# Weighted inputs of a bidirectional state-space scan: backward direction on ScalarE, forward on GpSimd

## The reference

```python
w_end = jnp.exp(cum[:, :, -1:] - cum) * dtc
states = jnp.einsum("bcjgn,bcjge,bcjgep->bcgepn", bc, w_end, xc)
chunk_decay = jnp.exp(cum[:, :, -1])
...
return h * dec[..., None, None] + st, h        # the scan over the chunks
```

## Time and profile before

| | |
|---|---|
| median of 3 runs | 1362.33 us (1358.07 to 1363.33) |
| profiled execution, device time | 1359.37 us |
| its span (first to last instruction) | 1357.5 us |
| mean granted clock of TensorE | 0.982 of full |
| busy: TensorE, VectorE, ScalarE, GpSimd | 1298.8, 545.5, 596.5, 603.1 us |
| the stage of the ten products | from 298.0 to 311.1 us of the span |

### The profile page before, as it was taken

The page is one execution under the profiler, slowest core; times in us unless marked ns, Lnnn a source line. Parts: engine busy times, 40 slices in busy tenths (PEclk is TensorE's granted clock), DMA queues, the critical chain, the costliest instruction groups (busy, mean ns, idle before and its releaser), DMA issues.

```text
span 1357.5 us, 17575 instructions
## 1 busy us (share of the span) xinstructions
PE 1298.8 (96%) x6464; PEld 1046.4 (77%) x6464; DVE 545.5 (40%) x1069; ACT 596.5 (44%) x961; POOL 603.1 (44%) x502
## 2 busy tenths in 40 slices
PE   8999999898989999999999899999899999999998
PEld 1688888666777888888888788767678888888886
DVE  2577652668445444443542362783520000001113
ACT  3712555767335344433323464785452222223231
POOL 0335232367143444444665732455424444445562
PEclk9999999999989999999999899999989999999999
DMA  9427457050233445454423312111202222222221
GB/s 393 172 88 285 169 164 133 1 187 1 77 141 124 185 185 193 185 216 179 155 93 98 135 64 92 56 30 57 93 32 93 93 96 106 107 93 93 93 93 62
DMA packets 27401, 166.76 MB, mean 123 GB/s; under 512 B 2976, under 2 KB 5280, under 8 KB 8656
## 3 DMA queue, kind: packets, MB, share of 16 engines
q1 hardware_dynamic: 25328, 151.31, 31.2%
q10 hardware_dynamic: 2016, 14.68, 2.9%
HBM read 163.85 MB, written 6.32 MB: 125 GB/s over the span
## 4 chain that ended last, share of the span: by engine, by line
PE 82%; DVE 7%; ACT 4%; DMA 3%; POOL 2%; issue 1%; SPq 0%; ACTq 0%; DVEq 0%; POOLq 0%
PE bank L274 53%; PE bank L333 12%; PE bank L310 6%; DMA ada_ring<-ada_dram 2%; PE bank L712 1%; PE bank L1349 1%; DVE ada_ring L1987 1%; PE bank L1321 1%; DMA w_raw<-w_dram 1%; PE bank L522 1%; DVE arena L2052 1%; PE bank L536 1%; POOL arena L940 1%; ACT arena L760 1%; PE bank L688 1%
## 5 line engine op out<-in xcount | busy, mean ns | idle before, releaser
L267 POOL TENSOR_TENSOR w_lo<-w_raw,w_hi 128x512 fp32r<-128x512 f32 x336 | 457.3, 1392 | 604.2 <-ACT w_hi L258 604.2
L274 PE MATMUL bank<-h_hi,w_hi 128*128 128x512 f32 x1120 | 442.3, 395 | 12.5 <-DVE h_lo L449 6.9
L274 PE MATMUL bank<-h_lo,w_hi 128*128 128x512 f32 x1120 | 439.2, 392 | 0.0
L274 PE MATMUL bank<-h_hi,w_lo 128*128 128x512 f32 x1120 | 439.0, 392 | 0.0
L258 ACT ACTIVATE w_hi<-w_raw 128x2048 fp32r<-128x2048 f32 x88 | 168.6, 1916 | 299.9 <-PE bank L274 177.1
L274 PEld LDWEIGHTS bank<-h_hi,w_hi 128*128 128x128 f32 x1120 | 212.3, 190 | 57.8 <-issue 8.1
L274 PEld LDWEIGHTS bank<-h_hi,w_lo 128*128 128x128 f32 x1120 | 212.3, 190 | 44.8
L274 PEld LDWEIGHTS bank<-h_lo,w_hi 128*128 128x128 f32 x1120 | 212.4, 190 | 43.0
L2316 DVE TENSOR_TENSOR arena<-arena,bank 128x512 f32 (+1 forms) x22 | 15.1, 687 | 210.2 <-PE bank L274 210.2
L2178 DVE TENSOR_TENSOR h_lo<-arena,h_hi 128x1024 fp32r<-128x1024 f32 x22 | 32.4, 1486 | 135.1 <-ACT h_hi L1813 123.6
L2006 DVE SCALAR_TENSOR_TENSOR arena<-bank,params,arena 128x511 f32<-128x511 f32 (+1 forms) x36 | 25.4, 704 | 136.0 <-ACT arena L1793 114.3
(11 more groups left out here) (276 smaller groups left out, 1756.4 us busy)
## 6 DMA issues: line engine op xcount, KB each, us to landing
w_raw<-w_dram SPq DMA_DIRECT2D x92, 1024.0 KB, 4.8
ada_ring<-ada_dram SPq DMA_DIRECT2D x30, 1024.0 KB, 4.8
ada_ring<-ada_dram ACTq DMA_DIRECT2D x14, 1024.0 KB, 4.9
arena<-ada_dram SPq DMA_DIRECT2D x4, 1024.0 KB, 10.1
arena<-x_dram SPq DMA_DIRECT2D x2, 2048.0 KB, 11.6
bias_copies<-bias_rows SPq DMA_DIRECT2D x1, 4096.0 KB, 17.4
arena<-bias_copies SPq DMA_DIRECT2D x4, 768.0 KB, 5.7
ada_ring<-rpb_dram SPq DMA_DIRECT2D x16, 128.0 KB, 9.5
```

Of the source, the lines that this page charges most:

```text
L267: last = nc.gpsimd.tensor_tensor(w_lo[b % 2][:, part], w_raw[b % 2][:, part], w_hi[b % 2][:, part], ALU.subtract)
L274: last = nc.tensor.matmul(bank[:, :], w[:, ft, k, :], x[:, k, :], start=k == first and m == 0, stop=k == final and m == 2)
```

## The change

GpSimd makes the forward products alone (five instead of ten). The backward ones are made by ScalarE at the head of `ssd_act`, one ACTIVATE for each head (128x64, Copy, with the head's weight column as scale), eight per chunk, 40 in all. A new semaphore `xw_back` counts them. TensorE's order of the ten groups is the same; it waits for `xw` or `xw_back` by the direction. ScalarE waits for `st` at 2k before it writes `xw[1]` again, and L1058 and all behind it follow the 40 instructions.

```diff
@@ ssd_pool
-            for n in range(10):
-                d, c = n % 2, ORDER[n % 2][n // 2]
-                if n >= 2:
-                    pool.wait_ge(sd["st"], n - 1)
-                w = wend[:, d, c * 8:(c + 1) * 8].unsqueeze(2).to_broadcast([P, 8, 64])
-                nc.gpsimd.tensor_tensor(heads(xw[d]), heads(xtok[:, c, :]), w, ALU.mult).then_inc(sd["xw"], 1)
+            for k in range(5):
+                c = ORDER[0][k]
+                if k:
+                    pool.wait_ge(sd["st"], 2 * k - 1)
+                w = wend[:, 0, c * 8:(c + 1) * 8].unsqueeze(2).to_broadcast([P, 8, 64])
+                nc.gpsimd.tensor_tensor(heads(xw[0]), heads(xtok[:, c, :]), w, ALU.mult).then_inc(sd["xw"], 1)
@@ ssd_pe
-                pe.wait_ge(sd["xw"], n + 1)
+                pe.wait_ge(sd["xw_back" if d else "xw"], k + 1)
@@ ssd_act
+            act.wait_ge(sd["wend"], 3)
+            for k in range(5):
+                c = ORDER[1][k]
+                if k:
+                    act.wait_ge(sd["st"], 2 * k)
+                for h in range(HEADS):
+                    part = slice(64 * h, 64 * h + 64)
+                    last = nc.scalar.activation(xw[1][:, part], xtok[:, c, part], ACT.Copy, scale=wend[:, 1, c * 8 + h:c * 8 + h + 1])
+                last.then_inc(sd["xw_back"], 1)
```

More of the change, by code:

```diff
@@ L202, in build @@
                                               "ptr", "pt_act", "pt_dve", "pv", "ohi", "olo")}
-        sd = {n: sem(f"ssd_{n}") for n in ("tr", "tok", "cs", "col", "wend", "xw", "st", "stf", "cb", "cbf", "bc",
+        sd = {n: sem(f"ssd_{n}") for n in ("tr", "tok", "cs", "col", "wend", "xw", "xw_back", "st", "stf", "cb", "cbf", "bc",
                                            "rows", "dmin", "dexp", "z", "t", "both", "m", "y", "yf", "yz", "sq", "mean", "root", "yn", "hi", "lo")}
```

## The result

The changed kernel takes 1364.68 us (median of 20 runs, 1360.97 to 1368.84), the kernel before 1360.80 us in 20 runs beside them. The ratio is 1.0025, with a 95% interval of 1.0015 to 1.0035: slower by 2.0 to 4.8 us, less than 0.5%. The profiled execution has a span of 1364.1 us, 6.6 us over that of the earlier trace rows, which is more than the medians say; the trace tells how much of it is the change's.

A forecast was written before the change was run, and what follows sets the result against it. GpSimd's products and TensorE's groups in turn were taken as the bound; a late start plus four turns of 3.19 us gave +3.1 us, so 1362.5 on the profiled time, 1365.4 on the median, forecast 1364.5 us, range 1360 to 1369.5.

The forecast's parts named there:

- the stage: From the start of the last L578 to the first decay instruction; the fifth backward group in it was forecast 3.1 us later.
- The product's price: Eight ScalarE ACTIVATEs of 128x64 for one backward product: 2.0 us, range 1.76 to 2.1.
- The turn: Backward cycle over the single buffer xw[1]: product 2.0, to TensorE 0.04, group 1.13, back 0.02, 3.19 us in all.
- The late start: ScalarE is free only at 298.29 us, so the first backward group starts at 300.33 instead of about 299.
- The forward turn: GpSimd's forward product, TensorE's group and the waits: 2.3 to 2.7 us, fitting inside 3.19 at no cost.
- The covers: L1058, moved behind the 40 ACTIVATEs, ends at 313.7 us, before the last group (314.2); no cost, cover 0.5 us.
- Rival A: ScalarE's product takes under 1.38 us, so VectorE limits these products: -1.0 us, 1358.4 to about 1361; chance 0.08.
- Rival B: Neighbouring ACTIVATEs on ScalarE do not overlap: product 2.73 us, +6.75 us, 1366 to 1369; chance 0.06.
- Rival C: TensorE's clock falls during these groups: +5.9 to +10.9 us, 1365 to 1370, up to 1373 on the median; chance 0.07.
- Rival D: The shift is swallowed in the chain behind these products: 1359.4 to 1362 us; chance 0.06.

The follow-up runs named there:

- e4: The changed kernel, but GpSimd makes the first backward product too and ScalarE the other four; stage 15.60 us, ratio 0.9983 to the kernel before.
- e3: The changed kernel with two buffers in turn for the backward products; stage 14.36 us, ratio 0.9995 to the kernel before.
- e11: The changed kernel with GpSimd making both first products and two backward buffers (e3 and e4 together); stage 13.22 us, ratio 1.0005 to the kernel before.
- e2: The changed kernel with one ACTIVATE of 128x512 per backward product instead of eight; stage 13.22 us, ratio 1.0000 to the kernel before.
- e8: The changed kernel with four more ACTIVATEs ahead of each backward product, 12 in all; stage 23.02 us, ratio 1.0047 to the kernel before.
- e1: The changed kernel with eight more ACTIVATEs ahead of each backward product, 16 in all; stage 30.34 us, ratio 1.0100 to the kernel before.
- e6: The kernel of e4 run once more; stage 15.60 us, ratio 0.9997 to the kernel before.
- e7: The changed kernel with GpSimd making both first products and two buffers for both directions; stage 14.16 us, ratio 0.9987 to the kernel before.
- e9: The kernel before with two ScalarE copies into dead buffers ahead of the first decay instruction; stage 15.21 us, ratio 1.0022 to the kernel before.

## Why the prediction was right, point by point

- *The forecast.* 1364.5 us, +3.1 us for the stage; measured 1364.68 us, +3.9 us between medians and +3.3 in the stage. The sign and the size hold, and that it stays under 0.5%. The agreement of the time to 0.2 us is luck: the forecast stood on some 1361.4 us for the kernel before, which is 0.6 over the 1360.80 measured now, and its difference was 0.8 under the measured one. That of the stage is not luck.
- *The product's price.* Taken 2.0 us from bounds of 1.76 and 2.1; measured 2.00 to 2.02. One instruction takes 335 ns in the mean (forecast 341), and neighbours start 0.24 us apart, by the overlap of L428 with L431 and not by that of L1068. ScalarE's groups by form between 300 and 320 us, columns as in the earlier trace rows:

```profile
L1065 ACT ACTIVATE arena<-arena,small 128x64 f32<-128x64 f32 x40 | 10.1, 335 | 4.9 <-PE bank L967 4.9
```

  The estimate from the rule of the Trainium skill ("ScalarE: Activation LUTs", What ACT_TABLE_LOAD costs), 332 ns alone and 239 in a row, agrees with these rows to 3 ns.
- *The turn.* Forecast 3.19 us, measured 3.24: 0.02 for the product, 0.02 for the group (1.15 where another follows), 0.01 for the waits. Four turns of 0.05 us more are the 0.2 us by which the stage is over the forecast.
- *The late start.* Forecast 1.3 us (300.33 against about 299); e4 gives 1.42.
- *The forward turn.* It was put at 2.3 to 2.7 us, with 1.5 us for a product beside VectorE as the mean of the first two (3.03/2). That reading was wrong: of two such products in e4, ahead of the stage as here, one takes 1.04 us and the other 2.03. In the stage a product takes 1.51 us (e3), so the figure was right by luck, and where ScalarE does not hold it up the forward direction's turn is 2.77 us (e3, e11). Both are under 3.24, so it costs nothing here.
- *The covers.* L1067 ends at 317.08, before the last group does (317.75), so L1067 costs nothing. The forward group lies right behind the backward one in TensorE's wait. VectorE's last add starts at 317.93 us, 0.5 ahead of the decay instructions. As said, GpSimd's and VectorE's idle time gives nothing back.
- *Rival A* would have been right below 1.38 us: e2, at 0.72, has VectorE in the chain. Its gain was put at 1.0 us and is 0.5, since VectorE's turn is 2.77 us and not the 2.65 of decay products that all take 0.69.
- *Rival B* fell: neighbours overlap.
- *Rival C* did not happen here but is real, and nearer than 0.07 may sound: e8 and e1 have it. Its price was put too low: a group takes 2.09 us and not 1.8, a ratio of 1.8 where the durations of two single L274 have 1.6; one matmul's duration was the wrong row for a group of them. The 5 us that it added for the products behind the stage had no row, and e1 and e8 do not have them: the part behind the stage is 1044.2 and 1045.4 us, against 1045.7.
- *Rival D* fell for the change itself (+3.3 us in the stage; +3.5 and +2.9 in the mean time of its two sets) and with e1 (+16.6 and +14.9). e8, with +9.29 and +7.0, leaves some 2 us unexplained. For shifts of 0.5 to 2 us e3, e4, e6 and e7 leave it open, since the clock elsewhere moves the time by as much.

## What to carry to other kernels

Before sharing a producer's work between two engines, write down the round trip of each, with the consumer's part in it if the buffer is single, and the moment at which the new engine is free; here 2.02 + 1.22 us per turn replaced 2 x 1.44, and the head start of GpSimd was lost. If the helper is slower than its share of the turn, give it the second buffer and leave the first item with the engine that is idle early (e11 gave back all 3.3 us of the stage). And look at what the next limit allows before spending more: VectorE had no idle time in most of the stage in e2, e11 and e7, and none of them came below 13.2 us.

## What the runs showed of the hardware

- A group of two fp32 products of 128x256 takes 1.10 (e2) to 1.17 us (e1) at the full clock and 2.09 us at 1.2 GHz (e1), and the low clock came in with TensorE waiting for 3.1 us between pairs of groups (e1) and for 2.2 us (e8), not with 1.2 us (the change, twice).
- GpSimd's 128x512 product takes 1.04 us alone and up to 1.35 (the change) or 1.5 us (e3) beside VectorE's decay products, and those go from 0.68 to 0.81 us, in single cases to 0.96 (e4), 1.16 (before), 1.34 (the change) and 1.55 (e7).
- Executions of the kernel before have a standard deviation of 2.3 to 2.9 us in each of three sets, and most of that goes with the mean granted clock: some 0.8 to 0.9 us for each 0.001, with correlations of -0.77 to -0.90. One kernel's stop near 400 us, from L394 to the next stop, costs 19.9 us in one profile of the change (403.19 to 423.12) and 21.5 in the other (400.61 to 422.12); the kernel before has 21.5 and e4 19.0. Two of the kernels made for this study (that of e4 and e6, and that of e7) had a mean clock 0.002 to 0.004 above that of the kernel before, over 12 runs in each set; a shift of the stage alone (e9) did not bring it about, and why they have it is open.
